# Two recurrences of a hybrid decoder: sample states read as split pairs, mixed features in a ring of two steps

## The reference

```python
def step(carry, xs):                       # mLSTM, layer A; the sums and gates are left out here
    s = jnp.einsum('bhtd,bhjd->bhtj', qc, kc) * jnp.exp(D - mt[..., None])
    num = w_inter[..., None] * jnp.einsum('bhvd,bhtd->bhtv', C, qc) + jnp.einsum('bhtj,bhjv->bhtv', s, vc)
    C_new = wC[..., None, None] * C + jnp.einsum('bhjv,bhjd->bhvd', vc * wk[..., None], kc)
...
def step(S, xs):                           # gated linear attention, layer C
    o = jnp.einsum('bhtd,bhdv->bhtv', qd, S) + jnp.einsum('bhtj,bhjv->bhtv', A, vc)
    S_new = jnp.exp(bL)[:, :, 0, :, None] * S + jnp.einsum('bhjd,bhjv->bhdv', kc * jnp.exp(bL - b), vc)
...
out = jnp.einsum('ble,ed->bld', mix, w_out)        # 2048 mixed features to 1024
y = x + _rmsnorm(out, post_g)
```

## Time and profile before

| | before |
|---|---|
| median of 3 runs | 2282.79 us (2282.31 to 2284.64) |
| the profiled execution | 2283.07 us, span 2281.3 us |
| PE busy | 2149.0 us, 94% of the span |
| DVE, ACT, POOL busy | 55%, 35%, 12% |
| recurrence A, 719 to 1170 us | 451 us, PE busy 417.5 |
| recurrence C, 1758 to 2281.3 us | 523 us, PE busy 492.9 |

### The profile page before, as it was taken

One profiled execution on the slowest core, in us unless ns is written; L12 is line 12 of the kernel. 1 busy time (PEld: TensorE's weight loads), 2 busy tenths in 40 slices (PEclk: granted clock), 3 DMA queues, 4 the chain that ended last, 5 costly groups with the idle time before them and its releaser, 6 DMA issues. The chain is left out here.

```text
span 2281.3 us, 32663 instructions
## 1 busy us (share of the span) xinstructions
PE 2149.0 (94%) x12758; PEld 1856.8 (81%) x12758; DVE 1260.8 (55%) x2183; ACT 792.1 (35%) x1441; POOL 284.5 (12%) x287
## 2 busy tenths in 40 slices
PE   5999999999996999999968999999997999999998
PEld 4999999999996667777648999999997566666665
DVE  5455576555565665555536557655665644444442
ACT  4455533322223433333335434212322522222222
POOL 3001100000000111111121000000000332323232
PEclk8999999999998999999979999999998899999999
DMA  2122232543335334444331332343233443434442
GB/s 97 58 66 64 66 100 74 169 132 93 98 114 182 110 115 154 130 130 129 87 117 58 88 95 86 132 160 114 86 105 114 172 164 138 160 139 158 149 130 65
DMA packets 204476, 262.23 MB, mean 115 GB/s; under 512 B 47584, under 2 KB 151264, under 8 KB 202288
## 3 DMA queue, kind: packets, MB, share of 16 engines
q1 hardware_dynamic: 204336, 260.30, 35.6%
HBM read 170.29 MB, written 89.97 MB: 114 GB/s over the span
## 5 line engine op out<-in xcount | busy, mean ns | idle before, releaser
L547 DVE TENSOR_TENSOR pa_stage<-pa_ps,pa_stage 128x536 f32<-128x536 f32 x110 | 77.1, 713 | 129.0 <-PE pa_ps L514 123.3
L547 DVE TENSOR_TENSOR pc_stage<-pc_ps,pc_stage 128x536 f32<-128x536 f32 x110 | 77.1, 712 | 104.6 <-PE pc_ps L514 91.1
L362 PE MATMUL pa_ps<-a_XT_hi,pa_w_hi 128*128 128x358 f32 x576 | 133.1, 339 | 0.3 <-PEq L197 0.3
L362 PE MATMUL pa_ps<-a_XT_hi,pa_w_lo 128*128 128x358 f32 x576 | 126.0, 327 | 0.0
L362 PE MATMUL pa_ps<-a_XT_lo,pa_w_hi 128*128 128x358 f32 x576 | 125.7, 326 | 0.0
L1279 PE MATMUL mc_ps<-mc_wout_hi,mc_mix_hi 128*128 128x512 f32 x288 | 119.1, 413 | 2.0 <-POOL mc_mix_lo L2816 1.4
L1279 PE MATMUL ma_ps<-ma_wout_hi,ma_mix_hi 128*128 128x512 f32 x288 | 120.9, 420 | 0.0
L1279 PE MATMUL ma_ps<-ma_wout_hi,ma_mix_lo 128*128 128x512 f32 x288 | 115.0, 399 | 0.0
L1279 PE MATMUL ma_ps<-ma_wout_lo,ma_mix_hi 128*128 128x512 f32 x288 | 114.8, 398 | 0.0
L1279 PE MATMUL mc_ps<-mc_wout_hi,mc_mix_lo 128*128 128x512 f32 x288 | 113.7, 395 | 0.0
L1279 PE MATMUL mc_ps<-mc_wout_lo,mc_mix_hi 128*128 128x512 f32 x288 | 113.1, 393 | 0.0
(11 more groups left out here) (503 smaller groups left out, 6102.3 us busy)
## 6 DMA issues: line engine op xcount, KB each, us to landing
pa_w_raw<-in_w_a SPq DMA_DIRECT2D x57, 512.0 KB, 4.6
pc_w_raw<-in_w_c SPq DMA_DIRECT2D x49, 512.0 KB, 4.6
scr_c<-pc_stage SPq DMA_DIRECT2D x48, 512.0 KB, 3.2
scr_a<-pa_stage SPq DMA_DIRECT2D x40, 512.0 KB, 3.2
ma_hin<-scr_a SPq DMA_DIRECT2D x32, 512.0 KB, 3.7
mc_hin<-scr_c SPq DMA_DIRECT2D x32, 512.0 KB, 3.7
mc_sample_state<-in_s SPq DMA_DIRECT2D x32, 512.0 KB, 4.6
out_s_s<-mc_sample_state SPq DMA_DIRECT2D x32, 512.0 KB, 2.7
```

The source lines that it names most:

```text
L362: ins = pe.matmul(self.ps[:, 3 * s + t, 0:TC], w[:, k, :], x[:, k, t * TC:(t + 1) * TC], start=(k == 0 and j == 0), stop=(k == KT - 1 and ...
L547: dve.tensor_tensor(dst, self.out(p, product), x, ALU.add).then_inc(self.added, 1)
```

## The change

Both recurrences get the same three things, and a few that follow from them.

1. **Split reads.** ACT rounds each sample state (`csh`) at the end of its step, DVE subtracts the rest (`csl`) at the end of its own. The masked queries hold hi in columns 0 to 31 and lo in 32 to 63. The read is four single-pass products with a 64-column stationary operand; rows 0 to 31 and 32 to 63 of the result are added later (in A in the small work of the group; in C ACT copies the low rows, DVE adds, and then ACT norms). POOL writes masked queries one unit at a time, as soon as the unit that used those columns has been read.
2. **A ring of two steps** of four feature tiles instead of 16 tiles (`OutRing` in place of `OutProjection`). The LRU's features are split two tiles a step instead of eight a chunk. In the last chunk hi and lo stand side by side in one stationary operand (columns 0 to 47 and 64 to 111), so two products serve where three did, and the two row blocks are added at the end.
3. **The post norm's addition** goes from POOL to DVE: the scaling writes back to PSUM, two additions of 128x512 write the output into the residual's own buffer. PE's first product of the next chunk waits for the additions (`out_read` counts two a chunk). The residual's load moves from h == 1 to h == 2, behind the store of that buffer.
4. **The first chunk** leaves out the products with the prompt's state, which is zero there.

In A the LRU tiles come in the first half of a step and the head's in the second; the LRU's load moves from h == 2 to h == 3 and two loads of sample heads four steps ahead. The core of the diff (unchanged waits and the second of two like places are left out):

```diff
+class OutRing:
...
+    def products(self, pe, ps, n, i, e, first, last, new_w):
...
+            if n < 8 * H:
+                for j, (m, w) in enumerate(((self.m_hi, w_hi), (self.m_hi, w_lo[:, cols]), (self.m_lo, w_hi))):
+                    ins = pe.matmul(ps[:, 6 + half, :], m[:, at, :], w, start=first and j == 0, stop=last and j == 2)
+            else:
+                for j, w in enumerate((w_hi, w_lo[:, cols])):
+                    ins = pe.matmul(ps[0:64 + LAST, 6 + half, :], self.m_hi[:, at, 0:64 + LAST], w,
...
+    def post_dve(self, dve, ps, c):
...
+        for half in range(2):
+            dve.scalar_tensor_tensor(out=ps[:, 6 + half, :], in0=ps[:, 6 + half, :], scalar=st[:, 4:5],
+                                     in1=self.post[:, half * 512:half * 512 + 512], op0=ALU.mult, op1=ALU.mult).then_inc(self.scaled, 1)
+        dve.wait_ge(self.x_in, 16 * c + 16)
+        for half in range(2):
+            cols = slice(half * 512, half * 512 + 512)
+            dve.wait_ge(self.scaled, 2 * c + half + 1)
+            ins = dve.tensor_tensor(self.yx[:, cols], ps[:, 6 + half, :], self.yx[:, cols], ALU.add)
+            ins.then_inc(self.out_read, 1)
...
+    def tail_act(self, act, ps, buf):
+        act.wait_ge(self.m_used, 4 * NC)
+        for half in range(2):
+            act.activation(buf[0:LAST, half * 512:half * 512 + 512], ps[64:64 + LAST, 6 + half, :], ACT.Copy).then_inc(self.tail_low, 1)
...
+    def tail_dve(self, dve, ps, buf):
...
+            dve.tensor_tensor(x, ps[0:LAST, 6 + half, :], x, ALU.add).then_inc(self.tail_sum, 1)
...
@@ stage_mix_a, SP's queue
                     if h == 1 and c:
                         O.store_y(sp, c - 1, P)
-                        O.load_x(sp, c, P if c < 8 else LAST, False)
-                    if h == 2 and c < 8:
+                    if h == 2 and c:
+                        O.load_x(sp, c, P if c < 8 else LAST)
+                    if h == 3 and c < 8:
                         load_hl(c + 1)
@@ stage_mix_a, PE's part_b
                     if n >= H:
                         pe.wait_ge(state_ready, n - H + 1)
-                    for d in range(2):
-                        pe.matmul(ps[0:rows, 2, 0:MV], hin[s][:, d, 0:rows], cst[:, h, d, :], start=(d == 0), stop=(d == 1))
+                        for d in range(2):
+                            pe.matmul(ps[0:rows, 2, 0:MV], hin[s][:, d, 0:rows], cst[:, h, d, :], start=(d == 0), stop=(d == 1))
@@ stage_mix_a, PE's out(n, half)
+                    if half == 0:
+                        pe.wait_ge(lru_ready, n + 1)
+                        if h == 0:
+                            pe.wait_ge(O.out_read, 2 * c)
+                    else:
+                        pe.wait_ge(mix_ready, n + 1)
@@ stage_mix_a, PE's unit
+                    pe.wait_ge(cs_lo_ready, u + 1)
...
-                        ins = pe.matmul(ps[0:NS, 2, 0:MV], qm[:, d, b * NS:(b + 1) * NS], cs[r][:, d, :],
-                                        start=(d == 0), stop=(d == 1))
+                        for j, x in enumerate((csh, csl)):
+                            ins = pe.matmul(ps[0:2 * NS, 2, 0:MV + 1], qm[:, d, 2 * b * NS:2 * (b + 1) * NS], x[:, d, :],
+                                            start=(d == 0 and j == 0), stop=(d == 1 and j == 1))
@@ stage_mix_c, ACT
+                def copy_sample_lows(g):
+                    act.wait_ge(os_done, g + 1)
...
+                    act.activation(gns[:], ps[NS:2 * NS, 2, :], ACT.Copy).then_inc(os_low, 1)
+
+                def norm_samples(g):
+                    act.wait_ge(os_sum, g + 1)
+                    root_of_mean(sqs_chain, 4, NS, gns[:], ps[0:NS, 2, :], g)
+                    act.activation(gns[:], gns[:], ACT.Copy, scale=sm[0:NS, 6:7]).then_inc(gns_ready, 1)
+
+                def sample_state_hi(u):
+                    act.wait_ge(s_in[u % SRING], 16 * (u // SRING) + 16)
+                    if u:
+                        act.wait_ge(read_done, u)
+                    act.activation(csh[:], cs[u % SRING][:], ACT.Copy).then_inc(cs_hi_ready, 1)
...
-                    if h == 0 and c:
-                        O.post_act(act, ps, c - 1, P)
                     u = unit_of(n - 1)
                     if u is not None and u % NSEQ == NSEQ - 1:
                         norm_samples(u // NSEQ)
+                    if h == 0 and c:
+                        act.wait_ge(c_done, n + 1)
+                        O.post_act(act, ps, c - 1, gn[:])
                     part_m(n)
+                    u = unit_of(n)
+                    if u is not None and u % NSEQ == NSEQ - 1:
+                        copy_sample_lows(u // NSEQ)
+                    if n < UNITS:
+                        sample_state_hi(n)
@@ stage_mix_c, PE's unit, first read of a group
-                        pe.wait_ge(gns_ready, g)
+                        if g:
+                            pe.wait_ge(sqs_chain, 3 * g - 2)
@@ stage_mix_c, DVE
+                def sum_samples(g):
+                    dve.wait_ge(os_low, g + 1)
+                    dve.tensor_tensor(gns[:], ps[0:NS, 2, :], gns[:], ALU.add).then_inc(os_sum, 1)
+
+                def sample_state_lo(u):
+                    dve.wait_ge(cs_hi_ready, u + 1)
+                    dve.tensor_tensor(csl[:], cs[u % SRING][:], csh[:].bitcast(F32), ALU.subtract).then_inc(cs_lo_ready, 1)
...
                     part_m(n)
                     if h == 0 and c:
-                        O.post_dve(dve, ps, c - 1, P)
+                        O.post_dve(dve, ps, c - 1)
+                    if u is not None and u % NSEQ == NSEQ - 1:
+                        sum_samples(u // NSEQ)
+                    if n < UNITS:
+                        sample_state_lo(n)
@@ stage_mix_c, POOL
-                    if u is not None and u % NSEQ == NSEQ - 1 and u + 1 < UNITS:
-                        masked_q((u + 1) // NSEQ)
+                    if u is not None and u < UNITS - NSEQ:
+                        next_q(u)
                     lo(n)
-                    if h == 0 and c:
-                        O.post_pool(pool, c - 1, P)
```

More of the change, by code:

```diff
@@ L1983, in _ @@
+                first_q()
                 for n in range(NSTEP):
-                    c, h, rows = where(n)
-                    if n % NSEQ == 0 and 0 < n < UNITS:
-                        masked_q(n // NSEQ)
+                    u = unit_of(n)
+                    lru_lo(n)
+                    if u is not None and u < UNITS - NSEQ:
+                        next_q(u)
                     lo_head(n)
-                    if h == 0:
-                        lo_hl(c)
-                        if c:
-                            O.post_pool(pool, c - 1, P)
@@ L1992, in _ @@
-                O.post_pool(pool, 8, LAST)
 A_POOL_LINKS = 13
@@ L2321, in stage_mix_c @@
         kw = [a.sb(f"mc_group_keys{s}", [K3, 256], F32R) for s in range(2)]
-        ss = [a.sb(f"mc_sample_scores{s}", [2 * NS, NS]) for s in range(2)]
+        ss = [a.sb(f"mc_sample_scores{s}", [2 * NS, 2 * NS]) for s in range(2)]
         gns = a.sb("mc_sample_normed", [NS, GV])
@@ L2500, in part_b @@
                         pe.wait_ge(state_ready, n - H + 1)
-                    for d in range(2):
-                        pe.matmul(ps[0:rows, 3, :], hin[n % 2][:, d, 0:rows], cst[:, h, d, :], start=(d == 0), stop=False)
+                        for d in range(2):
+                            pe.matmul(ps[0:rows, 3, :], hin[n % 2][:, d, 0:rows], cst[:, h, d, :], start=(d == 0), stop=False)
                     pe.wait_ge(sc_ready, n + 1)
@@ L2505, in part_b @@
                     for j, (x, v) in enumerate(((sh, vh), (sl, vh), (sh, vl))):
-                        pe.matmul(ps[0:rows, 3, :], x[0:rows, 0:rows], v[0:rows, :], start=False, stop=(j == 2))
+                        pe.matmul(ps[0:rows, 3, :], x[0:rows, 0:rows], v[0:rows, :], start=(n < H and j == 0), stop=(j == 2))
                     if n >= 2:
@@ L2525, in out @@
                     if h == 0 and half == 0:
-                        pe.wait_ge(O.out_read, c)
+                        pe.wait_ge(O.out_read, 2 * c)
                     pe.wait_ge(mix_ready, n + 1)
-                    for e in range(4 * h + 2 * half, 4 * h + 2 * half + 2):
-                        O.products(pe, ps, e, e == 0, e == 15, new_w)
+                    for i in range(2 * half, 2 * half + 2):
+                        e = 4 * h + i
+                        ins = O.products(pe, ps, n, i, e, e == 0, e == 15, new_w)
+                    if half:
+                        ins.then_inc(O.m_used, 1)
                 def unit(n, u):
                     g, b, r = u // NSEQ, u % NSEQ, u % SRING
-                    pe.wait_ge(s_in[r], 16 * (u // SRING) + 16)
+                    pe.wait_ge(qm_ready, 1)
                     if b == 0:
-                        pe.wait_ge(qm_ready, g + 1)
-                        pe.wait_ge(gns_ready, g)
+                        if g:
+                            pe.wait_ge(sqs_chain, 3 * g - 2)
```

(8 more changed lines are left out.)

347 lines of the change are left out of this document (248 added, 99 removed).

## The result

The change takes 2213.8 us (median of 4 runs, 2212.39 to 2216.84) against 2283.44 (4 runs, 2282.31 to 2284.64): a ratio of 0.9697, 95% interval 0.968 to 0.9714. The forecast was 2220, with a range of 2202 to 2246. In a later series it took 2214.84 (5 runs), a ratio of 0.9701 (0.9688 to 0.9715).

A forecast was written before the change was run, and what follows sets the result against it. TensorE was taken to bound both recurrences, busy 93 to 94%, with room on the other engines. Terms of 30.6 us in the first (A) and 32.5 in the second (C), together 63, took 2283 to 2220; range 2202 to 2246.

The forecast's parts named there:

- reads, 29 units: Sample-state reads become four single-pass products: 0.59 us saved a unit (17) in the first recurrence, 1.00 (29) in the second.
- the start: First four steps, without the empty state's products: 3.5 us saved in the first recurrence, 3 in the second.
- last chunk, products: Two products instead of three for 16 tiles x 2 halves in the last chunk: 7.4 us saved in each recurrence.
- chunk boundaries: Waits removed and added where one chunk meets the next: 3.5 us saved in the first recurrence, 6.1 lost in the second.
- tail: The last rows' addition moves to VectorE behind two copies and a sum: 0.8 us longer in each recurrence.
- A's boundaries: First recurrence's chunk boundaries: the update's 14.6 us wait goes, eight 1.4 us stalls on VectorE's adds (11.1) come, saving 3.5.
- C's boundaries: Second recurrence's chunk boundaries: 0.6 us lost at six, 1.6 at two behind a finished sample group, 0.7 regained: -6.1.
- Free boundaries: Rival, chance 0.13: VectorE's adds end before the next chunk's first product is due, stalls are regained: 2196 us.
- Worse boundaries: Rival, chance 0.20: VectorE's added work keeps the first recurrence's 14.6 us wait and lengthens the second's boundaries: 2244 us.
- A costly read: Rival, chance 0.04: the 64-column stationary operand or late data costs a read what a pass saves: 2270 us.
- Two subtractions in turn: Rival, chance 0.05: VectorE's state split and GpSimd's feature split hold each other in every step, the read waits: 2340 us.

The follow-up runs named there:

- the addition from SBUF: The change, with VectorE in the first recurrence scaling into an SBUF tile and adding the residual from there in one 128x1024 operation: 2211.41 us.
- three products: The change, with a third product for each tile and half put back in the last chunk: 2227.65 us.
- the GpSimd operation: The change, with an additional 128x1024 GpSimd operation, its output unread, at the first recurrence's eight chunk boundaries: 2211.73 us.

## Why the prediction was right

The forecast of 2220 missed the median by 6 us. Its terms, measured from the step lengths of one trace of each kernel (a boundary's gain is counted without the read's share):

```
term                     A forecast  measured     C forecast  measured
reads, 29 units                  17      20.3             29      31.7
the start                       3.5      -1.5              3       2.5
last chunk, products            7.4       7.3            7.4       7.1
chunk boundaries                3.5       5.8           -6.1      -2.5
tail                           -0.8      -0.4           -0.8      -0.4
sum                            30.6      31.5           32.5      38.4
```

The sum of A came out within 1 us by luck: misses of +3.3, -5.0 and +2.3 cancel. What carried the forecast are the reads and the last chunk, 66 of the 70 us, and they were right in their mechanism.

**The reads.** The step was right, and mis-sized by the row behind it: the forecast counted from product to update. The 0.1 us that the update itself got shorter, behind single-pass products, was missing: 3 us in each recurrence. The run with float32 reads brings the 0.1 back. That the wider stationary costs next to nothing (0.03 us), and that the split is covered in ordinary steps, came out as put.

**The start of A** is the step that failed, in sign too: 3.5 forecast, -1.5 measured. The condition was named (VectorE sets the pace there), but only as a limit to the gain. VectorE's step there got a subtraction of 0.80 and an idle 1.0 in front of it, in which it waits for ScalarE's rounding; but an idle 2.2, in which it waited for ScalarE's `ma_inter` before, is gone with the empty state's products. The runs say that the split's work is not where the time went. From the stage's first instruction to the transposes of step 3 it takes 63.08 us with the reads back in float32, 62.81 without the split as well, 63.07 before and 64.56 in the change. So rounding and subtracting cost 0.3 there beside float32 reads, and all that is new without the split, the products left out among it, brought 0.3; then 1.5 were lost with the cheaper reads, which were to bring 1.8. TensorE, with less to do, idled more and was granted less clock: 0.76 in the stretch from 733 to 783 us (first row), 0.86 in the same one before (second).

```profile
733.00:783.00 50.00, 38.95 (x152) 0.76 0.38 132
```

```profile
733.00:783.00 50.00, 39.98 (x170) 0.86 0.45 153
```

That the clock, and not only the wait, made this difference is argued from the stretches. Three runs with the same code at this place (the addition from SBUF, three products, the GpSimd operation) took 63.6 to 63.9 us for this part at a higher granted clock (about 0.76 for 0.73), but lost more than that in step 4 (12.07 or 12.08 for 10.39). The cause stays open.

**A's boundaries.** The wait that goes (14.6 us) was right; the wait that comes in its place was put at 11.1 (eight times the 1.46 from 893.44 to 894.9 would be 11.7) and is 8.1, since the two additions took 1.28 together and not 1.4 and began 0.1 before the scaling had ended. At steps 13 and 29, at full clock in both traces, the exchange brought 0.97 each. The group ends at 9 and 25, at full clock too, lost 0.4 each by the new wait of the transposes. The rest is the clock. In the kernel before, the boundary steps 5, 17 and 21 were granted 0.89, 0.80 and 0.89, in the change 1.00. The first five rows are steps 5, 9, 13, 17 and 21 before, the others 17, 21 and 33 of the change:

```profile
792.59:808.16 15.57, 13.49 (x64) 0.89 0.38 114
841.72:855.82 14.10, 12.01 (x57) 1.00 0.20 65
889.42:903.45 14.03, 11.95 (x64) 1.00 0.27 91
937.03:953.95 16.92, 14.84 (x57) 0.80 0.25 89
987.50:1002.99 15.49, 13.40 (x63) 0.89 0.36 114
```

```profile
926.02:939.80 13.78, 11.48 (x57) 1.00 0.21 68
971.33:983.69 12.36, 11.41 (x64) 1.00 0.33 113
1103.29:1114.31 11.02, 9.85 (x43) 0.85 0.26 79
```

The three took 1.5, 2.8 and 1.5 us longer than the like steps at full clock, 5.8 in all, as much as the whole term. The last boundary, step 33, lost 2.5 in the change, at 0.85; in the second trace of the change, at 1.00, it lost 1.2, and the group ends took 13.2 for 13.8, so that the term is 8.9 there. The forecast priced stalls by their idle time alone, and that the term came near it is luck. That GpSimd's work at the boundary made the update late is shown by the rows: in the kernel before, the LRU's split held the first operation of the divide chain (1.64 for 0.16), the addition the second (2.27). In the change neither is held; with the addition put back one is (1.91), and TensorE waits for the state again, 7.1 of the former 14.6 us. The two in sequence in a kernel otherwise like the change were not run.

**C's boundaries** were overpriced: 0.3 us at an ordinary one for 0.6, 0.9 behind a group for 1.6. The chain was the one described, and the read waited 3.6 us, not about 5. Counted from the features' transposes (2007.63 before, 1962.25 in the change) GpSimd's scaling moved by 2.05 us, where 2.4 was put; and from its start to the read takes 3.40 (1970.98 to 1974.38), where it took 4.79: waiting for the Square alone saves 1.4 of the chain, where the difference between 2.4 and 1.6 allowed it 0.8.

**The rivals.** Free boundaries: no, 8.1 us of waits in A and 7.1 in C stand in the table. Worse boundaries: no, the wait of A's update for the state is gone. A costly read: no, by the row with 64 columns. Two subtractions in turn: each subtraction of C lasts 1.41 us on average instead of 1.23, so they do meet, but that is 0.2 us a step on an engine that had several to spare. A whole second one was covered in ordinary steps. The rule quoted from the Trainium skill ("SBUF — State Buffer", Who interferes with whom), that a VectorE instruction with two SBUF inputs contends with a GpSimd instruction that reads SBUF, is borne out by the 1.41.

## What to carry to other kernels

When a step's time is taken out of one engine by giving work to others, look for the stretches where those others already set the pace (here the weight splits at the start and the chunk boundaries): new work can show there, however much idle time the average shows. A second subtraction, hidden whole in ordinary steps, cost 4.3 of its 4.9 us in the first steps of C. Price a stall of TensorE with what follows it: 3.6 us of waiting cost 5.3, because the clock was at its lower level for a while afterwards; of A's seven waits of 2.1 us before, three stand in steps with a lowered clock. And when a wait remains, ask what stands ahead of the awaited instruction on its engine; moving it ahead of a copy was worth 10 us and took no work away.

## What had not been expected of the hardware

The two single-pass products of A's update took 0.1 us longer behind a float32 read than behind a single-pass one (0.35 for 0.25 from the update's start to the next product, and the 0.35 again in the run with float32 reads). GpSimd's operation of 128x1024 took 1.89 us with the same tile as both inputs and 2.73 with two tiles beside VectorE's subtraction; 2.35 had been seen before.
